# Hybrid decoder step with a gathering expert layer: four raw weight tiles, stages that open with gathering turns, gates as tanh

## The reference, cut to what matters

```python
h = rms_norm(x, n_mix_pre) * (1.0 + sc1) + sh1
bg, cg, hin, q, k, v, r, ga, gb, alow = jnp.split(h @ w_in, points, axis=-1)
y_conv, new_buf = short_conv(cg * hin, conv_buf, conv_w, conv_b)
branch_a = (bg * y_conv) @ w_proj_a
# branch_b: gated linear attention over q, k, v, r, alow, then @ w_proj_b
merged = jax.nn.sigmoid(ga) * branch_a + jax.nn.sigmoid(gb) * branch_b
x = x + g1 * rms_norm(merged @ w_out, n_mix_post)
h = rms_norm(x, n_ffn_pre) * (1.0 + sc2) + sh2
# PEER: for each token, 8 heads, the 16 best of 128 x 128 experts by two product keys
s = jnp.einsum('thpd,hpkd->thpk', (h @ wq).reshape(...), subkeys)   # two top-16 lists, their sums, top 16
act = jax.nn.gelu(jnp.einsum('thkd,td->thk', u_tab[expert], h))
out = jnp.einsum('thk,thkd->td', gate * act, v_tab[expert])
x = x + g2 * rms_norm(out, n_ffn_post)
```

## Time and profile before

| | |
|---|---|
| median of 3 runs | 4787.77 us (4781.85 to 4799.57) |
| the profiled execution | 4796.1 us, span 4794.3 us |
| busy, share of the span | PE 70%, DVE 55%, PEld 36%, POOL 35%, ACT 17% |
| DMA, mean | 292 GB/s, 1400.13 MB |
| mean granted TensorE clock | 0.772 of full speed |
| stages of part 0 | 835 to 1380 us |
| stages of part 1 | 1388 to 2470 us |
| stages of part 2 | 2482 to 3745 us |
| last_phase | 3760 to 4794 us |

### The profile page before, as it was taken

One profiled execution on the slowest core, in us unless ns is written; L12 is line 12 of the kernel. 1 busy time (PEld: TensorE's weight loads), 2 busy tenths in 40 slices (PEclk: granted clock), 3 DMA queues, 4 the chain that ended last, 5 costly groups with the idle time before them and its releaser, 6 DMA issues. The chain is left out here.

```text
span 4794.3 us, 46337 instructions
## 1 busy us (share of the span) xinstructions
PE 3340.5 (70%) x15679; PEld 1703.1 (36%) x15679; DVE 2624.4 (55%) x7543; ACT 805.6 (17%) x1284; POOL 1669.0 (35%) x1379
## 2 busy tenths in 40 slices
PE   8688996864358676586658856758666666677676
PEld 2578885864225444152115533314300011111111
DVE  0355345315865354577866444557688555555555
ACT  1222222323112211311001311121100001000000
POOL 0311100643225444354325534434333333333332
PEclk9789988986669888697779978769866666666666
DMA  6211111544369898998879988999899899999998
GB/s 248 87 36 37 46 38 36 168 147 136 150 247 367 319 352 329 372 380 347 314 275 404 405 326 343 394 361 398 334 355 362 354 408 404 406 409 416 404 415 353
DMA packets 243428, 1400.13 MB, mean 292 GB/s; under 512 B 30661, under 2 KB 47685, under 8 KB 100986
## 3 DMA queue, kind: packets, MB, share of 16 engines
q0 software_dynamic: 156672, 1140.92, 59.5%
q1 hardware_dynamic: 86522, 256.22, 14.8%
HBM read 1345.59 MB, written 51.43 MB: 291 GB/s over the span
## 5 line engine op out<-in xcount | busy, mean ns | idle before, releaser
L999 DVE CUSTOM_DVE_ANT_0 peer_uv<-peer_uv,all_PS 128x512 f32<-128x512 f32 x2176 | 1435.7, 685 | 1172.3 <-DMA peer_uv<-in_uv,peer_idx 762.6
L938 PE MATMUL all_PS<-peer_hT,peer_sel 96*128 96x512 bf16 x2176 | 1012.6, 489 | 1111.4 <-DVE peer_halves L999 914.6
L921 POOL DMA_INDIRECT peer_uv<-in_uv,peer_idx x1088 | 1060.7, 975 | 1800.8 <-PE all_PS L957 1408.3
L938 PEld LDWEIGHTS all_PS<-peer_hT,peer_sel 96*128 96x128 bf16 x2176 | 203.3, 103 | 2095.1 <-DVE peer_halves L999 1679.6
L957 PE MATMUL all_PS<-peer_uv,peer_zw 128*32 128x512 f32 x4352 | 881.4, 857 | 2.7 <-DVE peer_zw L1019 2.7
L809 POOL TENSOR_TENSOR flow_w_lo<-flow_w,flow_w_hi 128x1024 fp32r<-128x1024 f32 (+1 forms) x204 | 459.5, 2258 | 505.7 <-ACT flow_w_hi L802 503.4
L973 ACT ACTIVATE peer_ge<-peer_pre 128x4 f32<-128x4 f32 x272 | 55.6, 205 | 2119.0 <-DVE peer_pre L1005 2027.1
L829 PE MATMUL all_PS<-mix_h_hi,flow_w_hi 128*128 128x384 f32 (+1 forms) x672 | 278.5, 414 | 31.7 <-POOL flow_w_lo L809 31.7
L802 ACT ACTIVATE flow_w_hi<-flow_w 128x1024 fp32r<-128x1024 f32 (+1 forms) x204 | 203.7, 1004 | 435.8 <-DMA flow_w<-in_w_proj_a 118.3
L831 PE MATMUL all_PS<-mix_h_hi,flow_w_lo 128*128 128x384 f32 (+1 forms) x672 | 225.7, 336 | 0.0
L830 PE MATMUL all_PS<-mix_h_lo,flow_w_hi 128*128 128x384 f32 (+1 forms) x672 | 225.6, 336 | 0.0
(11 more groups left out here) (277 smaller groups left out, 4800.1 us busy)
## 6 DMA issues: line engine op xcount, KB each, us to landing
cond_w<-in_w_ada SPq DMA_DIRECT2D x12, 2048.0 KB, 8.0
flow_w<-in_w_gate_ab SPq DMA_DIRECT2D x48, 512.0 KB
flow_w<-in_w_query SPq DMA_DIRECT2D x48, 512.0 KB
flow_w<-in_w_conv SPq DMA_DIRECT2D x36, 512.0 KB
peer_uv<-in_uv,peer_idx POOLq DMA_INDIRECT x1088
gla_w<-in_w_heads SPq DMA_DIRECT2D x24, 512.0 KB, 3.7
flow_w<-in_w_proj_b SPq DMA_DIRECT2D x24, 512.0 KB
flow_w<-in_w_out SPq DMA_DIRECT2D x24, 512.0 KB
```

Source lines behind the costliest of these rows:

```text
L921: self.nc.gpsimd.indirect_dma_start(out=self.uv[:, n % self.NUV, :], out_offset=None, in_=self.A["uv"], in_offset=bass.IndirectOffsetOnAxi ...
L938: nc.tensor.matmul(PS[:, f, :], self.sel[:, c:c + 1].broadcast_to([3 * GR, P]), self.hT[:, g % self.NH, f * 512:(f + 1) * 512], start=True ...
L999: nc.vector.tensor_tensor_reduce(part, part, PS[:, f, :], 1.0, 0.0, ALU.mult, ALU.add, self.halves[:, d, f, e:e + 1]).then_inc(M["dotted"], 1)
```

## The change

- `Stream` has four raw slots in place of two: `bring(i)` waits for the low part of tile i - 4.
- In mix, merge, out and keys the gathering turns of `turns.before()` stand ahead of the splits on ACT and DVE (PE and POOL had them first already; in part 0's mix POOL does too now). SP does them after the first two groups of the input.
- To make room in SBUF: the input of mix comes in four groups of two chunks, where there were two of four; that of merge in eight groups of one, where there were four of two. keys has two slots for its raw input instead of one for each block, so the third block waits for the first split. NH is 5, not 6. The tile `merged` is gone: its sum is made in `sig`, and so SP's load of the next gates (`gates(d)`, d >= 2) waits for the store of chunk d - 2, where it waited for that chunk's sum on DVE. `tmp` of norm has one slot, `s2` of keys lies in the raw input, `iota` is shorter.
- The gates: ACT computes tanh of half the logit, merge adds 1 in the multiplication, and out halves the result on ACT, since sigmoid(z) = (1 + tanh(z/2)) / 2.

```diff
-    def __init__(self, sc, sources, raws=2, pairs=4):
+    def __init__(self, sc, sources, raws=4, pairs=4):
...
-    NUV, NZ, ND, NH, AHEAD = 10, 3, 4, 6, 4
+    NUV, NZ, ND, NH, AHEAD = 10, 3, 4, 5, 4
... mix_phase
-        h = Halves(sc, "h", KD, n, lambda g: A["h1"][part.index, :, 4 * g:4 * g + 4, 0:n], 4)
+        h = Halves(sc, "h", KD, n, lambda g: A["h1"][part.index, :, 2 * g:2 * g + 2, 0:n], 2)
 sync:
-            for g in range(h.groups):
+            for g in range(h.slots):
                 h.fetch(sp, g)
...
+            gat.turn(sp, turns.before())
+            for g in range(h.slots, h.groups):
+                h.fetch(sp, g)
             if w0 == 0:
                 w.start(nc, sp=sp)
-            gat.turn(sp, turns.before())
 scalar:
+            gat.gelu(act, turns.before())
             for g in range(h.groups):
                 h.make_high(nc, act, g)
...
-            gat.gelu(act, turns.before())
...
-                        nc.scalar.activation(sig[:, d % 2, q, :], bank(j), ACT.Sigmoid).then_inc(a_out, 1)
+                        nc.scalar.activation(sig[:, d % 2, q, :], bank(j), ACT.Tanh, scale=0.5).then_inc(a_out, 1)
 vector:
+            gat.dots(dve, turns.before())
             for g in range(h.groups):
                 h.make_low(nc, dve, g)
-            gat.dots(dve, turns.before())
... merge_phase (its ACT and DVE reordered in the same way, as are those of out and keys)
-        o = Halves(sc, "o", KD, n, lambda g: A["ob"][part.index, :, g, :, 0:n], 2)
+        o = Halves(sc, "o", KD, n, lambda g: A["ob"][part.index, :, g // 2, g % 2:g % 2 + 1, 0:n], 1)
...
                 if d >= 2:
-                    sp.wait_ge(done, d - 1)
+                    sp.wait_ge(saved[d % 2], 16 * (d // 2))
...
                     sp.wait_ge(done, d + 1)
-                    sp.dma_start(A["merged"][part.index, :, d, 0:n], merged[:, d % 2, :]).then_inc(saved[d % 2], 16)
+                    sp.dma_start(A["merged"][part.index, :, d, 0:n], sig[:, d % 2, 0, :]).then_inc(saved[d % 2], 16)
                     if d + 2 < KD:
                         gates(d + 2)
... keys_phase
             for i, u in enumerate(part.tiles):
-                sp.dma_start(raw[:, i], A["h2"][u]).then_inc(h_in[i], 16)
+                if i >= 2:
+                    sp.wait_ge(low, i - 1)
+                sp.dma_start(raw[:, i % 2], A["h2"][u]).then_inc(h_in[i], 16)
```

More of the change, by code:

```diff
@@ L1112, in _ @@
         def _(pool):
+            gat.fetch(pool, turns.before())
             if w0 == 0:
                 w.start(nc, pool=pool)
-            gat.fetch(pool, turns.before())
             for j in range(NJ):
@@ L1234, in gates @@
                 if d >= 2:
-                    sp.wait_ge(done, d - 1)
+                    sp.wait_ge(saved[d % 2], 16 * (d // 2))
                 sp.dma_start(sig[:, d % 2], A["sig"][part.index, d, :, :, 0:n]).then_inc(sig_in[d % 2], 16)
-            for g in range(o.groups):
+            for g in range(o.slots):
                 o.fetch(sp, g)
@@ L1241, in _ @@
             gat.turn(sp, turns.before())
+            for g in range(o.slots, o.groups):
+                o.fetch(sp, g)
             for j in range(NJ):
@@ L1365, in _ @@
                 act.wait_ge(G["m_mm"], part.m_before + j + 1)
-                nc.scalar.activation(m_rows[0:part.rows[i], i, q * WC:(q + 1) * WC], bank(j), ACT.Copy).then_inc(m_out, 1)
+                nc.scalar.activation(m_rows[0:part.rows[i], i, q * WC:(q + 1) * WC], bank(j), ACT.Copy, scale=0.5).then_inc(m_out, 1)
                 if i == nt - 1:
@@ L1533, in keys_phase @@
         R, nt = part.rows, len(part.tiles)
-        raw = sc.sb("raw", [P, nt, KD, P])
+        raw = sc.sb("raw", [P, 2, KD, P])
         h_hi, h_lo = sc.sb("h_hi", [P, KD, n], F32R), sc.sb("h_lo", [P, KD, n], F32R)
@@ L1592, in _ @@
         def _(act):
+            gat.gelu(act, turns.before())
             for i in range(nt):
                 act.wait_ge(h_in[i], 16)
-                nc.scalar.activation(h_hi[:, :, part.at[i]:part.at[i] + R[i]], raw[:, i, :, 0:R[i]], ACT.Copy).then_inc(high, 1)
-            gat.gelu(act, turns.before())
+                nc.scalar.activation(h_hi[:, :, part.at[i]:part.at[i] + R[i]], raw[:, i % 2, :, 0:R[i]], ACT.Copy).then_inc(high, 1)
             for j in range(NJ):
@@ L1623, in _ @@
                 dve.wait_ge(high, i + 1)
-                nc.vector.tensor_tensor(h_lo[:, :, here], raw[:, i, :, 0:R[i]], h_hi[:, :, here].bitcast(F32),
+                nc.vector.tensor_tensor(h_lo[:, :, here], raw[:, i % 2, :, 0:R[i]], h_hi[:, :, here].bitcast(F32),
                                         ALU.subtract).then_inc(low, 1)
-            gat.dots(dve, turns.before())
             for j in range(NJ):
                 gat.dots(dve, turns.upto(j))
+                if j == 2:
+                    dve.wait_ge(low, nt)
                 if 2 <= j:
@@ L1919, in hybrid_decoder @@
         G = {"PS": top.ps("PS", [P, 8, 512])}
-        for name, shape in (("ones", [P, P]), ("ident", [P, P]), ("iota", [P, NK]), ("eps", [P, 1]), ("one", [P, 1]),
+        for name, shape in (("ones", [P, P]), ("ident", [P, P]), ("iota", [P, TOPK]), ("eps", [P, 1]), ("one", [P, 1]),
                             ("carry", [P, CC, CW - 1])):
```

31 lines of the change are left out of this document (13 added, 18 removed).

## The result

| | before | after |
|---|---|---|
| median time, 6 runs each on one chip | 4792.35 us (4781.85 to 4803.23) | 4816.79 us (4808.45 to 4823.86) |
| profiled execution / its span | 4796.1 / 4794.3 us | 4808.45 / 4806.6 us |
| table loads on ACT, traced | 158 | 116 |
| mean granted TensorE clock | 0.772 | 0.777 |

The change made the kernel slower: ratio 1.005, 95% interval 1.0031 to 1.0069, that is 24 us. The forecast was 4.5 us the other way. The traces have 18 table loads more on either side than the 140 and 98 given with the change; the difference, 42, is the same.

A forecast was written before the change was run, and what follows sets the result against it. Gathers on DMA bound last_phase; in parts 1 and 2 only idle DMA time could change. Terms -3 + 5.5 - 20 - 5 + 15 + 3 = -4.5 us gave 4791.6 us profiled, 4783 median; 8-in-10 range 4735 to 4825.

The forecast's parts named there:

- keys term: Keys 0: with input in smaller pieces the third block's load waits for a round trip, +2.5 us.
- gates as tanh: ACT loses 42 table loads; gain only in mix 1's gates, -5 us, between 0 and -14.
- turns first, third block in keys: Stage starts: DVE handles tokens while input lands, -20 us (bounds 0 and -45); keys 0's third block +2.5.
- smaller pieces, one h slot less: Extra input round trips cost +7 us in merge 0, +3 in mix 0; one h slot less costs +3.
- store before the gates: Merge, parts 1 and 2: waiting for the landed store delays ACT's weight, +15 us; bounds 0 and +55.
- four slots, with merge 0's pairs: Four raw weight slots: -3 us in the bodies of mix's first half, out and keys; -7 in merge 0.
- Rival B: Merge 1 and 2: the store's full landing, 4 to 5 us a pair, +55 instead of +15; 4823 us, chance 0.13.
- my term: Merge's store wait: weight reaches ACT 14 to 15 us after the store, +1.3 us x 12 pairs = +15.
- Rival C: Merges, mixes and keys: extra pieces land in 7 to 8 us under gathers, not 4; +25, 4808 us, chance 0.13.
- The h slot: One h slot less: SP waits once more for a spread at five places, +3 us, between 0 and +12.
- the other case: Merge: if the store had to wait for gathers issued earlier, four of 2.6 us would make 10 us.

The follow-up runs named there:

- e4: The kernel before with the gates as tanh alone; 4787.7 us, ratio 1.0001.
- e3: e2 with merge's and mix's input in larger pieces again and six h slots; 4766.0 us, ratio 0.9952.
- e2: e1 with merge's own tile for the sum again, so the gates' load waits for the sum, not the landed store; 4800.8 us, ratio 1.0025.
- e1: The changed kernel with two raw slots again; 4837.4 us, ratio 1.011.
- f1: The kernel before with one edit: merge's gates' load waits until the store of the sum has landed; 4824.2 us, ratio 1.0066.
- f2: The changed kernel with the sum in the input's dead raw pieces, so the gates' load waits for the sum again; 4780.4 us, ratio 0.9981.
- f3: e3 with the sum in the room of the raw pieces and three raw weight slots; 4751.4 us, ratio 0.9919.
- h1: f3 with weights brought one product earlier in merge, mix, out and keys, plus the change's store wait, sum in the gates' tile; 4722.9 us, ratio 0.9855.

## Why the prediction was wrong

The chain of experiments beside the terms of the sum (medians; the five measured figures add up to the change by construction). The keys term, +2.5, stands with the turns first, since e3 still has it:

| part | forecast | measured | by |
|---|---|---|---|
| gates as tanh | -5 | -4.2 | e4 |
| turns first, third block in keys | -17.5 | -21.7 | e3 - e4 |
| smaller pieces, one h slot less | +13 | +34.8 | e2 - e3 |
| store before the gates | +15 | +36.6 (34 and 36 in other settings) | e1 - e2; f1; after - f2 |
| four slots, with merge 0's pairs | -10 | -20.6 (-20 in f2) | after - e1 |
| sum | -4.5 | +24.9 (24.4 beside its own runs of before) | |

*Two steps failed, by 22 us each: the store's price, +1.3 us x 12 pairs, and the smaller pieces, to which I gave +10 us in part 0 and nothing in parts 1 and 2.* For the store the mechanism was right: the load for ACT is late by the store's landing, and ACT's wait is on the path. Two sizes were wrong. The landing was taken as 4.1 us, worked out from a load; it is 4.8 to 7.0 us in merge 1 and 2.3 to 7.7 in merge 2. And I let the smaller queue ahead of weight and gates give back most of it, down to 1.3 us. It gave back about half: the weight came 2.3 us later, and the store's period in merge 1 went from 16.5 us to 19.0, 2.5 us a pair. Merge 1 paid 17.1 us (177.4 against f2's 160.3), 2.9 us for each of its six waits, merge 2 6.3, about the 1.3 us of my term (9.0 and 10.7 in the other two settings), and merge 0, to which I gave next to nothing for this wait, 6.5 (69.1 against 62.6): its pairs of 5.3 us have no cover for a landing. These sum to 30 of the 36 us. With two slots, where merge 0's pairs wait for a slot anyway, it paid only 1 to 2 us. Rival B had the right place and sign. Its threshold (weight later than about 17 us after the store) was not reached, at 15.1 us, and the price in merge 1 still came out at 2.9 us a pair. I had argued against it that DMA is busy for 92% of the stretch in the earlier trace rows. From the first to the seventh store it was 90%, and it fell to 78%, before and after:

```profile
1679.11:1775.79 96.68, 73.30 (x366) 45.23 (x368) 50.08 (x127) 11.12 (x18) 45.72 (x36) 0.87 0.90 346
```

```profile
1670.24:1783.81 113.57, 76.52 (x366) 46.34 (x368) 50.13 (x127) 11.26 (x19) 45.75 (x36) 0.82 0.78 292
```

So a share of nine tenths was no proof that lost time is made up.

*Pieces.* In mix 0 I gave the round trip 3 us (3.7 by the spans of e2 and e3) and in merge 0 two of them 7 (2.6); in the merges and in mix 1 and 2 of the later parts I let it vanish inside the gain of the turns first. There it cost 24 us by the same spans: merge 1 8.9, mix 2 8.5, merge 2 5.9, mix 1 0.6. Until the last split is done DVE takes no further token, PE gives no buffers back, and DMA then runs dry, as at mix 2 above. There I had seen only half: the block that ACT must empty was in the text (-3 for the stage), that the second piece's request stands behind it was not. Rival C (round trips of 7 to 8 us under gathers, +25) had the size; its reason holds for the first trip of a stage (the reloads reached ACT 8.2 us after the request in mix 2, 8.4 in merge 2), not for the two that follow in merge, 3.6 us each. The last split came 24.2 us after the start in merge 1 and 24.4 in merge 2, where the text put it at 21. For keys the refetch of the third block was priced at what the turns gain; the traces agree roughly (keys 0 +3.1 us, forecast +2.5) and no run here tried it alone. The h slot was forecast at +3 and is not measurable.

*Slots.* Where the text said they would do nothing, they did nothing (merge 1), and merge 0's pair came to the forecast size once the store did not wait (5.3 us). Elsewhere 3 us was too little. Three pairs of profiles differ by the slots (e1 and after, e2 and f2, e3 and f3 with three): in all three merge 0 is shorter, by 5, 10 and 11 us, and mix 0, which the text did not single out, by 7, 2 and 4. Neither stage carries gathers. The rest is spread over other stages, keys 2 first (6, 10 and 2), in amounts by which untouched stages vary from run to run (keys 2 reads 562 to 573 us over these kernels); where it lies stays open.

*What held.* Turns first, in size and in its signs (L999 ahead of L866, idle DMA at out 2 from 14.0 to 6.4 us, out 1 and out 2 shorter by 5.0 and 4.1 us against 5 and 6); the tanh (42 loads fewer, nothing in mix 2 that stands out); `last_phase` unchanged. For the store the text gave 14 to 15 us as the sign for my term and 17 for B; ACT's wait read 16 to 17 and the weight came 15.1 us behind the store, so the two readings, for which I had one number, pointed to different cases.

On the store the trace agrees with the Trainium skill (DMA: Bandwidth & Descriptors, Queues, rings and completion order): engines taking turns between their queues let a small store past the gathers, and its 4.8 us landing is far from the 10 us of the other case. The 17.5 us in h1 came behind loads of its own queue. On the table loads the Trainium skill (ScalarE: Activation LUTs, What ACT_TABLE_LOAD costs) would have made 5 us more of gain. By e4's interval, 0.9988 to 1.0015, a gain of 5 us is possible and one of 10 is not; by the medians, 4 us and sure to about 7, both are.

A reading of the earlier trace rows was off without bearing on the sum: from the twelfth figure on it has 247 to 416 GB/s, with a dip to 275, not 300 to 419. No term that the runs can tell from nothing had the wrong sign: two costs and one gain were sized at half or less, and the costs were the larger.

## What to carry to other kernels

Before a wait for a landed store is put on a queue that also brings what others need, list what is behind it and give it the whole landing, unless a request made earlier takes its place; here DMA that was nine tenths busy gave back only about half of it. In this kernel room was won at no price that shows by using a buffer that was already dead (f2), while small input pieces cost 26 to 35 us and the wait for a store 34 to 37. More raw buffers gave 15 to 21 us, and asking for each weight one product sooner gave 44 more on three of them. Four slots with the sooner requests were not tried, since they do not fit with the large pieces.

## What the runs showed of the hardware

A 192 KB store issued among gathers landed in 4.8 to 7.0 us in merge 1 and 2.3 to 7.7 in merge 2 of the changed kernel, and in up to 17.5 with loads of its own queue ahead of it (h1); a 384 KB load landed in 8.5 (median of the gates' loads in merge 1). At merge 2's start the first reload of a pair of pieces reached ACT 8.4 us after the request, with the DMA engines at least 98% busy; the next two trips of load, ACT, DVE and request took 3.6 us each, at 34 to 50%.
